# Order of the high and low matmuls in the channel-major projections of a two-block transformer step

## The reference

```python
proj = h @ w_in[l]
x = x + jnp.concatenate([o_a, o_b], axis=-1) @ w_out[l]
a = h @ w_gate
return (jax.nn.silu(a) * (h @ w_up)) @ w_down
...
mk, mv = jnp.split(mem @ w_mem_kv, 2, axis=-1)
u = h @ w_in[i]
k, v = jnp.split(h @ w_kv, 2, axis=-1)
y = mixed @ w_out[i]
```

## Time and profile before

| what | value |
|---|---|
| median of 3 runs | 2058.97 us (2056.91 to 2059.02) |
| the profiled execution's own time | 2058.91 us |
| its span, first to last instruction | 2057.2 us |
| mean granted clock of TensorE | 0.993 |
| busy: PE, PEld, DVE, ACT | 98%, 84%, 60%, 42% of the span |
| DMA | 393.22 MB, 191 GB/s on the mean |

### The profile page before, as it was taken

How to read it: one execution, slowest core, us unless ns; L and a number is a source line. 1 busy time by engine, 2 the same in 40 slices (tenths; PEclk the granted TensorE clock), 3 DMA queues, 4 the chain that set the end, 5 groups by cost and what they waited for, 6 DMA issues and landing times.

```text
span 2057.2 us, 24840 instructions
## 1 busy us (share of the span) xinstructions
PE 2017.6 (98%) x10835; PEld 1737.6 (84%) x10835; DVE 1232.7 (60%) x1077; ACT 870.5 (42%) x807; POOL 26.3 (1%) x59
## 2 busy tenths in 40 slices
PE   7999999999999999999999999999899999999996
PEld 6888988888888888888888888888888888888884
DVE  6666554555666664456666546657756754566655
ACT  5444454444544443334444345343433433334532
POOL 2000000000000000000000000000000000000001
PEclk9999999999999999999999999999999999999998
DMA  9745444374655655565655756755585655544551
GB/s 335 232 164 184 139 168 143 131 278 167 212 189 180 204 178 192 189 199 183 202 176 195 264 187 211 229 156 181 171 304 185 211 197 187 184 144 143 205 189 57
DMA packets 295128, 393.22 MB, mean 191 GB/s; under 512 B 6286, under 2 KB 225227, under 8 KB 293355
## 3 DMA queue, kind: packets, MB, share of 16 engines
q1 hardware_dynamic: 292320, 365.19, 54.1%
q0 software_dynamic: 2240, 26.28, 3.2%
q10 hardware_dynamic: 459, 0.16, 0.0%
HBM read 383.22 MB, written 8.39 MB: 190 GB/s over the span
## 4 chain that ended last, share of the span: by engine, by line
PE 93%; DVE 4%; ACT 1%; issue 1%; DMA 1%; SPq 0%; DVEq 0%; ACTq 0%
PE G L378 37%; PE G L382 18%; PE G L423 11%; PE G L424 11%; PE G L425 11%; PE SB L649 2%; DVE hl_ring L348 1%; ACT hl_ring L345 1%; PE OB L670 1%; DMA xt<-in_x 1%; DVE ytmp L602 0%; DVE ringscr L1601 0%; PE OB L673 0%; PE TB L941 0%; PE TB L963 0%
## 5 line engine op out<-in xcount | busy, mean ns | idle before, releaser
L348 DVE TENSOR_TENSOR hl_ring<-raw,hl_ring 128x2048 fp32r<-128x2048 f32 (+1 forms) x348 | 784.0, 2256 | 531.1 <-ACT hl_ring L345 530.7
L345 ACT ACTIVATE hl_ring<-raw 128x2048 fp32r<-128x2048 f32 (+1 forms) x348 | 655.3, 1886 | 592.0 <-PE G L425 320.4
L378 PE MATMUL G<-ahl,hl_ring 128*128 128x512 f32 x2112 | 665.2, 396 | 0.0
L382 PEld LDWEIGHTS G<-ahl,hl_ring 128*128 128x128 f32 x2112 | 396.7, 188 | 93.7
L382 PE MATMUL G<-ahl,hl_ring 128*128 128x256 f32 x2112 | 415.1, 278 | 0.0
L378 PE MATMUL G<-ops,hl_ring 128*128 128x512 f32 x1216 | 384.3, 397 | 1.3 <-DVE hl_ring L348 1.3
L378 PEld LDWEIGHTS G<-ahl,hl_ring 128*128 128x128 f32 x2112 | 322.0, 189 | 0.8 <-issue 0.5
L382 PEld LDWEIGHTS G<-ops,hl_ring 128*128 128x128 f32 x1216 | 228.4, 188 | 53.9
L382 PE MATMUL G<-ops,hl_ring 128*128 128x256 f32 x1216 | 239.1, 278 | 0.0
L378 PEld LDWEIGHTS G<-ops,hl_ring 128*128 128x128 f32 x1216 | 185.6, 189 | 1.8 <-DVE hl_ring L348 1.5
L423 PE MATMUL G<-hl_ring,hhl 128*128 128x512 f32 x352 | 136.9, 389 | 0.0
(11 more groups left out here) (313 smaller groups left out, 1814.3 us busy)
## 6 DMA issues: line engine op xcount, KB each, us to landing
raw<-in_w_in SPq DMA_DIRECT2D x120, 1024.0 KB, 5.4
raw<-in_w_out SPq DMA_DIRECT2D x48, 1024.0 KB, 5.2
raw<-in_w_ffn_gate SPq DMA_DIRECT2D x44, 1024.0 KB, 5.0
raw<-in_w_ffn_up SPq DMA_DIRECT2D x44, 1024.0 KB, 5.0
raw<-in_w_ffn_down SPq DMA_DIRECT2D x40, 1024.0 KB, 5.1
raw<-in_w_kv_shared SPq DMA_DIRECT2D x24, 1024.0 KB, 5.0
raw<-in_w_mem_kv SPq DMA_DIRECT2D x16, 1024.0 KB, 5.1
ahl<-memop_scratch POOLq DMA_DIRECT2D x2, 4096.0 KB, 14.3
```

The costliest lines, as they stand in the source:

```text
L345: eng.activation(hi[:, s, 0:size], raw[:, r, 0:size], ACT.Copy).then_inc(hi_ready, 1)
L348: eng.tensor_tensor(lo[:, s, 0:size], raw[:, r, 0:size], hi[:, s, 0:size].bitcast(F32), ALU.subtract).then_inc(lo_ready, 1)
L378: eng.matmul(G[:, 2 * pair + b, :], hi[:, s, w], p.rhs(k), start=first and q == 0, stop=False)
L382: last = eng.matmul(G[:, 2 * pair + b, 0:TOK], lo[:, s, w], p.rhs(k)[:, 0, :], start=False, stop=final and q == len(ks) - 1)
```

## The change

In form A the loop over two entries at a time is gone. For each (block, slice) in the same list the 512-column matmul is issued and right behind it the 256-column matmul of the same block into the same bank, then the other block's two. Names, semaphores, tiles, the set of matmuls and their operands are the same, and so are the start and stop marks of each bank. Forms F and N are untouched, and the programs of ACT, DVE, SP and GpSimd are the same but for line numbers (which fall by 4).

```diff
             else:
                 order = [(mats[0], q) for q in range(len(mats[0][1]))]
-            for g in range(0, len(order), 2):
-                for (b, ks, width, col, first, final), q in order[g:g + 2]:
-                    kt, k = ks[q]
-                    w = slice(kt * width + col, kt * width + col + P)
-                    eng.matmul(G[:, 2 * pair + b, :], hi[:, s, w], p.rhs(k), start=first and q == 0, stop=False)
-                for (b, ks, width, col, first, final), q in order[g:g + 2]:
-                    kt, k = ks[q]
-                    w = slice(kt * width + col, kt * width + col + P)
-                    last = eng.matmul(G[:, 2 * pair + b, 0:TOK], lo[:, s, w], p.rhs(k)[:, 0, :], start=False,
-                                      stop=final and q == len(ks) - 1)
+            for (b, ks, width, col, first, final), q in order:
+                kt, k = ks[q]
+                w = slice(kt * width + col, kt * width + col + P)
+                eng.matmul(G[:, 2 * pair + b, :], hi[:, s, w], p.rhs(k), start=first and q == 0, stop=False)
+                last = eng.matmul(G[:, 2 * pair + b, 0:TOK], lo[:, s, w], p.rhs(k)[:, 0, :], start=False,
+                                  stop=final and q == len(ks) - 1)
             return last
```

## The result

The changed kernel takes 2064.38 us (median of 7 runs, 2063.77 to 2065.52); the kernel before, measured beside it, 2057.40 us (7 runs, 2056.91 to 2059.02). The ratio is 1.0033 with a 95% interval of 1.0022 to 1.0045: slower by about 7 us. The profiled execution took 2065.16 us with a span of 2063.4 us, 6.2 us over the span of before. The forecast was 2064.8 us.

A forecast was written before the change was run, and what follows sets the result against it. PE was taken as the bound, running end to end on a full queue. The profiled 2058.91 us plus one term, 1696 groups x 0.0035 = +5.9 us, gave 2064.8 us; range 2053 to 2076 us.

The forecast's parts named there:

- PE is the bound, and nothing else pays: Whole kernel: PE, busy 98% of the span, runs from a full queue; time is a sum of distances between matmul starts.
- No instruction, load, wait or release changes its price by itself: Form A tiles: same instructions, waits and bank releases, weight loads equally covered; these parts cost nothing.
- the 13.3 ns above the columns: Uniform runs of 512s or 256s: each matmul pays 13.3 ns beyond its columns' time, for the change of weights.
- Neighbours in one bank cost nothing: Form A: consecutive matmuls into one bank cost nothing extra, as form F's 0.2266 us average leaves no room for it.
- A fixed 1.7 ns for each change of size: Form A: four size changes per group instead of two, 0.0035 us more for each of 1696 groups, +5.9 us.
- flat: Form A rival: price by size alone, a group of four stays 0.6967 us, no change, 2059 us; chance 0.30.
- the lost discount: Form A rival: a 256 between two 512s pays 0.1200 us instead of 0.115, +16.8 us, 2075.7 us; chance 0.17.
- the smooth case: Form A rival: alternating sizes cost the uniform sum, 0.6932 us a group, -5.9 us, 2053.0 us; chance 0.12.
- The row that spoke for the step: Entry of `ffn0`: the first two 512s take 0.45 us, later pairs behind 256s 0.46 or more; favours counting size changes.

The follow-up runs named there:

- e4_cross: Changed kernel, sizes still alternating, but one block's 512-column matmuls interleaved with the other block's 256-column ones, in different banks: 2061.10 us, 1.0019 of before.
- e2_runs4: Changed kernel with form A issued as four 512-column matmuls, then four of 256 columns: 2064.45 us, 1.0032 of the kernel before.
- e5_lead3: Changed kernel, but each form A phase's first tile has three pairs between a doubled 512 and a doubled 256: 2055.32 us, 0.9990 of before.
- e1_runs16: Changed kernel with all 16 matmuls of 512 columns in a form A tile issued before its 16 of 256: 2055.68 us, 0.9991 of before.

## Why the prediction was right, and which step was not

*PE is the bound, and nothing else pays.* Right. But for the 1.1 us of clock at `out0`, the difference lies in distances between matmuls of form A; the waits of PE for weights and the busy times of DVE and ACT stand where they stood. (Of the 4.8 us of waits that the text puts "after the start", 3.5 are in `mem_k0`, at the start; nothing hangs on it.)

*No instruction, load, wait or release changes its price by itself.* Right as far as the traces show. The uniform prices didn't move: 0.2267 us from start to start in `down0` and `down1` before, 0.2268 after, and 0.120 in `pool` in both. That the 13.3 ns above the columns are paid for the change of weights is a reading that no run tests.

*Neighbours in one bank cost nothing.* Right, by the earlier trace rows and then by e4_cross, where different banks gave both rhythms at the same prices.

*A fixed 1.7 ns for each change of size, 0.7002 us for a group.* This step failed. No steady phase had that price. Groups cost 0.6934 us in `in_f` and `in_q` and 0.7066 in `ffn0`, and e2_runs4 refuted the rule by its sign. The sum came out because 1696 groups were divided between a price 3.3 ns below the old one and a price 9.9 ns above it. By the count of tiles that is 126 x 8 x 0.0099 - 86 x 8 x 0.0033 = +7.7 us. By their starts and ends the 15 phases from `in_f` on give +7.3, since tiles behind interruptions don't hold a full rhythm, and the clock at `out0` takes 1.1 of that away; with some tenths elsewhere the trace has +6.2. 6.2 us is 3.7 ns for a group on the mean, where the step had 3.5. Nothing known at the time said how they would divide; e5_lead3 shows that with another entry the same changed order is slightly faster than before (0.9990, at most 0.9999). So the time and the sign were right by luck, for the mechanism under them was not.

*Stretch by stretch.* The text gave four values for `ffn0` by which to judge: 246.5 for the forecast, 245.2 flat, 248.7 for the lost discount, 244.0 for the smooth case. It came out at 248.7, and at 244.1 in e5_lead3. Two rivals that I took to exclude each other are both right in size, each in its stretches. The reason that I gave for the dear one was wrong for the most part. By the starts in the traces of `ffn0` a 512 costs 233 ns before and 236 on the mean in the slow rhythm (by turns 233, 241 and 236), and a 256 goes from 115 ns to 117, not to 120. So two thirds of what a pair costs more is the 512's. In the fast rhythm (`in_q`) they cost 231.5 and 115. That surplus and debt "meet at once" there, as the smooth rival has it, is not shown.

*The row that spoke for the step.* That a 512 is dearer behind 256s was read rightly from the entry of `ffn0`, and e1_runs16 confirms it. But behind a run of sixteen 256s it lasts for five matmuls, and it is not a price per change. It was the sign of a stream that remembers, and the next thought should have been that a stream with a memory can have more than one steady state.

What stays open is what inside the chip keeps the rhythm. In the trace of the changed kernel, from 640 to 645 us (slow) and from 88 to 93 (fast), all weight loads but one start 2 to 5 ns behind the start of a matmul, and they show no wait. I didn't separate weight loads from moving data in an experiment. Open too is why streams behind attention steps fall either way.

## What to carry to other kernels

When PE is the bound, cost a change of order from start to start, and in several phases, not one; here a mean over the program hid a gain in some phases and a larger loss in others. An order in which sizes alternate can settle in more than one rhythm, so judge it by how each phase is entered, and if the entries can't be controlled prefer an order whose price hardly differs between phases, as that of before or runs of sixteen here. A rule fitted to one steady price and its difference from a uniform run is a fit to a single point: ask what a third order would cost before trusting it.

## What was not expected of the hardware

The same 32 matmuls of a tile, in the same order, in fp32r, with 128 x 128 weights loaded for each, take 8 x 0.6933 or 8 x 0.7067 us at the same full clock, and whichever it is holds for 44 tiles in a row. The fast rhythm costs what uniform runs of both sizes would (2 x 0.2267 + 2 x 0.1200 = 0.6934). One doubled 256 can make a whole phase 4.7 us shorter: entered from form F, `ffn0` turned when it came 3, 6 or 15 pairs after a doubled 512, and not with 1, 2 or 4. And in `ffn0` runs of four (0.7016 us for every four matmuls in e2_runs4) cost more than runs of two (0.6967) or sixteen (0.6957).
